# Two blocks of a language model in one kernel: the order of transposes and logits in both attention stages

## The reference, cut to what matters

```python
logits = einsum('bqhd,bqkhd->bhqk', qb, kg) * scale      # (+ bias or forget term in block 2)
logits = where(valid, logits, -inf)
p      = softmax(logits)                                   # kind c: one more term, the sink, in the sum
out    = einsum('bhqk,bqkhd->bqhd', p, vg)
```

## Time and profile before

| what | value |
|---|---|
| median of three runs | 981.58 us |
| the profiled execution | 983.36 us, of which the span (first to last instruction) is 981.6 us |
| mean granted TensorE clock | 0.952 of full |
| PE busy | 865.4 us, 88% |
| DVE busy | 503.7 us, 51% |
| ACT busy | 388.2 us, 40% |
| POOL busy | 81.4 us, 8% |
| attention rounds of stage 1 | about 158 to 231 us of the span |
| attention rounds of stage 2 | about 601 to 731 us of the span |

### The profile page before, as it was taken

The page is one execution under the profiler, slowest core; times in us unless marked ns, Lnnn a source line. Parts: engine busy times, 40 slices in busy tenths (PEclk is TensorE's granted clock), DMA queues, the critical chain, the costliest instruction groups (busy, mean ns, idle before and its releaser), DMA issues.

```text
span 981.6 us, 14775 instructions
## 1 busy us (share of the span) xinstructions
PE 865.4 (88%) x5993; PEld 716.8 (73%) x5993; DVE 503.7 (51%) x781; ACT 388.2 (40%) x523; POOL 81.4 (8%) x105
## 2 busy tenths in 40 slices
PE   4899998999996896668666699999989999999996
PEld 4899798999984441333312499988878799999995
DVE  5798667645655210111100644455557557666674
ACT  5333544464322111111111625545552356656462
POOL 1122001120000000000000000211115000000000
PEclk9999999899998898898888689999999999999998
DMA  6755463244569699999999736443352827564711
GB/s 205 258 184 196 147 233 112 87 172 172 172 252 424 279 423 422 422 422 422 422 421 353 135 122 161 162 140 118 118 141 86 288 81 254 170 214 139 242 47 43
DMA packets 93875, 217.50 MB, mean 222 GB/s; under 512 B 16455, under 2 KB 43973, under 8 KB 81537
## 3 DMA queue, kind: packets, MB, share of 16 engines
q1 hardware_dynamic: 93137, 215.32, 60.8%
q10 hardware_dynamic: 576, 1.18, 0.4%
q0 software_dynamic: 112, 0.30, 0.3%
HBM read 215.44 MB, written 1.34 MB: 221 GB/s over the span
## 4 chain that ended last, share of the span: by engine, by line
PE 63%; DMA 16%; DVE 10%; ACT 4%; issue 3%; SPq 3%; POOL 0%; DVEq 0%; ACTq 0%
PE ps L742 15%; PE ps L744 15%; PE ps L743 14%; DMA moe_ring<-in_w_expert_in 14%; PE ps L1045 6%; PE ps L979 5%; DVE w_lo L1408 3%; ACT w_hi L1130 1%; DMA stage<-in_w_in 1%; PE ps L904 1%; PE ps L958 1%; DMA stage_b<-in_w_up 1%; PE ps L889 1%; SPq L623 1%; PE ps L994 1%
## 5 line engine op out<-in xcount | busy, mean ns | idle before, releaser
L742 PE MATMUL ps<-x_hi,w_hi 128*128 128x256 f32 x1008 | 290.8, 288 | 6.3 <-DVE w_lo L1408 4.3
L743 PE MATMUL ps<-x_lo,w_hi 128*128 128x256 f32 x1008 | 287.8, 285 | 0.0
L744 PE MATMUL ps<-x_hi,w_lo 128*128 128x256 f32 x1008 | 287.7, 285 | 0.0
L742 PEld LDWEIGHTS ps<-x_hi,w_hi 128*128 128x128 f32 x1008 | 196.3, 195 | 9.2 <-DVE w_lo L1408 5.7
L743 PEld LDWEIGHTS ps<-x_lo,w_hi 128*128 128x128 f32 x1008 | 196.1, 195 | 0.3
L744 PEld LDWEIGHTS ps<-x_hi,w_lo 128*128 128x128 f32 x1008 | 195.9, 194 | 0.0
L1408 DVE TENSOR_TENSOR w_lo<-stage,w_hi 128x2048 fp32r<-128x2048 f32 (+2 forms) x72 | 162.1, 2291 | 56.1 <-ACT w_hi L1130 54.4
L1130 ACT ACTIVATE w_hi<-stage 128x2048 fp32r<-128x2048 f32 (+2 forms) x74 | 133.1, 1849 | 63.1 <-PE ps L744 55.8
L979 PE MATMUL ps<-moe_ring,qk 128*32 128x512 f32 x448 | 72.5, 739 | 41.4 <-DMA moe_ring<-in_w_expert_in 41.4
L979 PEld LDWEIGHTS ps<-moe_ring,qk 128*32 128x32 f32 x448 | 17.2, 131 | 82.5 <-DMA moe_ring<-in_w_expert_in 47.9
L742 PE MATMUL ps<-w_hi,x_hi 128*128 128x512 f32 (+2 forms) x176 | 66.5, 378 | 3.4 <-DVE x_lo L1415 1.8
(11 more groups left out here) (306 smaller groups left out, 1412.1 us busy)
## 6 DMA issues: line engine op xcount, KB each, us to landing
moe_ring<-in_w_expert_in SPq DMA_DIRECT2D x56, 1024.0 KB, 18.6
stage<-in_w_in SPq DMA_DIRECT2D x24, 2048.0 KB, 7.9
moe_ring<-in_w_expert_out SPq DMA_DIRECT2D x16, 1024.0 KB, 21.3
stage_b<-in_w_up SPq DMA_DIRECT2D x12, 1024.0 KB, 8.0
stage<-in_w_down SPq DMA_DIRECT2D x11, 1024.0 KB, 5.2
stage<-in_w_up SPq DMA_DIRECT2D x10, 1024.0 KB, 9.2
up_odd<-in_w_expert_in SPq DMA_DIRECT2D x8, 1024.0 KB, 26.9
down_odd_a<-in_w_expert_out SPq DMA_DIRECT2D x8, 1024.0 KB, 21.8
```

Of the source, the lines that this page charges most:

```text
L742: mm(out, still[0], moving[0], start=first, stop=False)
L743: mm(out, still[0], moving[1], start=False, stop=False)
L744: return mm(out, still[1], moving[0], start=False, stop=last)
```

## The change

In both loops of `schedule()` the step pt(h-1) now stands ahead of qk(h):

```diff
     for h in range(HEADS + 1):
+        if h >= 1:
+            at("pt", h - 1)
         if h < HEADS:
             at("qk", h)
-        if h >= 1:
-            at("pt", h - 1)
         if h == 1:
             at("mix", 2)
             at("mix", 3)
@@
     for h in range(heads + 1):
+        if h >= 1:
+            at("pt", HEADS + h - 1)
         if h < heads:
             at("qk", HEADS + h)
-        if h >= 1:
-            at("pt", HEADS + h - 1)
         if h < heads and gates:
             steps.append(gates.pop(0))
```

## The result

| | before | after |
|---|---|---|
| median of seven runs each | 982.79 us | 988.58 us |
| ratio, with 95% interval | | 1.0057 [1.0042, 1.0071] |
| profiled execution (span) | 983.36 us (981.6) | 987.48 us (985.8) |
| forecast | | 986.0 us, +0.45% (range 983.2 to 989.0) |

The ratio gives a loss of 5.6 us (4.1 to 7.0). The interval reaches to both sides of the 0.5% inside which I had put the larger chance; 0.40 stood for slower. The median lies 2.6 us over the forecast; 1.2 us of that is the median of the kernel before, which was 981.58 us in three runs and is 982.79 in seven. The two profiled executions differ by 4.1 us, nearly the 4.45 us of the sum.

A forecast was written before the change was run, and what follows sets the result against it. Both stages were taken as bound by PE with few gaps, a longer chain becoming stage 2's bound. 0.25 + 4.3, less 0.1, gave +4.45 us on the 981.58 us median: 986.0 us, range 983.2 to 989.0.

The forecast's parts named there:

- The closed loop: Stage 2, kind c: chain between odd heads' transposes becomes the bound, 17.14, 16.87, 16.88 and 17.27 us.
- The extra turn of the tile shape: Stage 2, PE: one more tile-shape turn a round, 0.17 to 0.18 us; 1.26 us over rounds 1 to 7.
- Stage 1: Round 4: PE's new wait for POOL, less the removed wait for the copy, nets +0.25 us without building up.
- the wait of 1.07 us: Stage 1, round 4: PE waits 1.07 us for POOL's normalized head 3 before its transposes.
- Stage 2: From the first logits to head 15's transposes: extra turns, then the longer chain, together +4.3 us.
- Carried to the end in full: After head 15's transposes, everything to the end shifts by the full loss; stage 1's 0.25 us likewise delays expert loads.
- The rival that the turn is free: Stage 2: the extra turn costs nothing, so +2.5 us in all, 984.1 us; chance 0.14.
- the rival of a gain: Both stages: copy waits of 1.2 us go and the new wait doesn't come, 980.4 us; chance 0.08.
- the four waits: Stage 2: PE waits for POOL before the transposes four times, 0.8 to 1.2 us each.
- the rival of the clock: Stage 2: new waits halve PE's clock, 994 us, or 988 with one spell; chance 0.14 with any other slow slip.

The follow-up runs named there:

- act_copy_last: Changed kernel, but ACT alone copies the transposes behind the next head's exponentials as before; ratio to the kernel before 1.0064 [1.0042, 1.0086].
- after_split_apart: Changed kernel with the two weight-split halves one before each gate fill in both stages; ratio to the kernel before 1.0013 [0.9997, 1.0028].
- ab_rounds_only: Kernel before with the new order in rounds 1 to 7 of stage 2 only; ratio to the kernel before 1.0023 [1.0008, 1.0038].
- best_candidate: Kernel before with ACT's copy first in both stages and split halves one before each gate fill in stage 2 only; 979.65 us against 983.10, 0.9965.
- after_split_stage2: Changed kernel with the split halves one before each gate fill in stage 2 only; ratio to the kernel before 1.0003 [0.9994, 1.0013].
- after_again: The changed kernel measured again, no edit; ratio to the kernel before 1.0059 [1.0039, 1.0079].
- stage2_only: Kernel before with the new order in stage 2 alone; ratio to the kernel before 1.0060 [1.0040, 1.0081].
- act_copy_first: Kernel before, but ACT alone copies the transposes ahead of the next head's exponentials; ratio to the kernel before 0.9991 [0.9977, 1.0005].
- split_apart_act_first: Kernel before with ACT's copy first and split halves one before each gate fill in both stages; ratio to the kernel before 0.9985 [0.9972, 0.9998].
- split_apart_stage2: Kernel before with only the split halves one before each gate fill in stage 2; ratio to the kernel before 1.0024 [1.0012, 1.0036].
- stage1_only: Kernel before with the new order in the first loop (stage 1) only; ratio to the kernel before 1.0007 [0.9994, 1.0020].

## Why the prediction was right, point by point

- **The closed loop** (POOL, transposes, logits, DVE's mask, split, next head) was forecast at 68.16 us over four turns and took 732.56 - 664.66 = 67.90. The last turn was 0.18 us shorter than I had it (17.09 for 17.27), of which I had taken off 0.1. The way from the first logits to the transposes of head 7 was 63.02 us, for 664.58 - 601.46 = 63.12. The chain as the bound is shown by act_copy_last (a longer link, a longer loop) and after_split_apart (a shorter link, no wait).
- **The extra turn of the tile shape**, the term with no row of its own, was taken at 0.18 us a round. It is 0.18 to 0.19 (rounds 2 to 7 of ab_rounds_only, and the 2.65 us between best_candidate and after_split_stage2). I counted one too many: of rounds 1 to 7 only six have it, which is why they cost 1.17 us and not 1.26. The Trainium skill, TensorEngine Tiling (Array Packing), Key Properties, says that changing the tiling mode drains TensorE. The trace agrees: a group of another shape starts 0.07 us before the end of the last one, one of the same shape 0.24 us.
- **Stage 1**: forecast +0.25, D1 shows +0.26 to +0.28. POOL's chain was right to 0.01 us; the wait of 1.07 us was not, since PE came up to 1.1 us later to that point than I had it. What PE lost ahead of the point it did not wait there, so the sum came out all the same.
- **Stage 2**: forecast +4.3, D2 shows +3.95 to +3.99.
- **Carried to the end in full**: in the profiled executions the rest from the transposes of head 15 took 253.19 us before and 253.24 us after. For the 0.25 us of stage 1 this isn't shown: from the transposes of head 7 to the first logits of stage 2 the 13 executions take 370.7 to 373.5 us (before 372.69, after 372.01), a spread ten times as large.
- **The rival that the turn is free** fell with ab_rounds_only, and the rival of a gain with the four waits. In the rival of the clock I judged the rounds right: from 675 to 730 us the granted clock is 1.00 in all four kernels with the loop (after, after_again, stage2_only, act_copy_last).
- **Where I misjudged**: that rows 11 show how much the clock stands at the end of stage 2. That was one execution. Of the 13 in the table it fell there in six: stage2_only, ab_rounds_only, act_copy_last, act_copy_first, split_apart_act_first and split_apart_stage2. In stage2_only (PE, PEld, DVE, ACT, POOL, granted clock):

```profile
732.00:734.00 2.00, 1.44 (x4) 0.69 (x4) 0.00 (x0) 0.31 (x1) 0.00 (x0) 0.66 0.18 64
734.00:736.00 2.00, 0.98 (x5) 1.00 (x5) 0.43 (x1) 1.93 (x2) 0.00 (x0) 0.50 0.00 0
736.00:738.00 2.00, 2.00 (x12) 2.00 (x11) 1.60 (x1) 2.00 (x2) 0.00 (x0) 0.50 0.00 0
738.00:740.00 2.00, 2.00 (x13) 2.00 (x13) 1.38 (x2) 0.16 (x1) 1.75 (x1) 0.64 0.00 0
```

and in the changed kernel at the same place:

```profile
732.00:734.00 2.00, 0.67 (x4) 0.49 (x5) 0.43 (x1) 0.54 (x2) 0.41 (x1) 1.00 0.77 290
734.00:736.00 2.00, 0.98 (x6) 0.61 (x6) 0.43 (x1) 1.25 (x2) 0.00 (x0) 1.00 0.00 0
736.00:738.00 2.00, 2.00 (x19) 2.00 (x18) 0.93 (x1) 2.00 (x2) 0.00 (x0) 1.00 0.00 0
```

Between 736 and 738 us the first does 12 matmuls, the second 19. The rest of the span is 253.0 to 253.5 us where the clock stands. Where it fell it is 254.8 to 255.8, and 257.5 in split_apart_stage2, whose last av waits 1.7 us longer. That is about 2 us, in kernels with the old and the new order alike.

**What stays open.** The stages account for 4.2 us, the timed runs show 5.6 (4.1 to 7.0), and the two repeats of the stage 2 order as much, so some 1.4 us may be real. The runs of one kernel spread over 2 to 6 us. The fall of the clock at the end of stage 2 is worth 2 of them, the stretch between the stages up to 2.8. The mean clock of the timed runs points to the clock for a part. A straight line through the 23 runs of the kernel before (0.946 to 0.955, 985.98 to 980.32 us) gives 0.48 us for 0.001 of mean clock. The 12 repeats lie 0.0017 lower, so an estimate from these numbers is 0.8 us. It doesn't settle the matter: within the seven first runs of the changed kernel a lower clock does not go with a longer time, and why the clock should fall more often in this kernel, no run shows.

## What to carry to other kernels

When a wait moves ahead of work that another engine needs, look for the closed chain it makes and add up its links over one turn. If the sum exceeds the turn of the bounding engine, the chain becomes the bound, and each link in it, even on an idle engine, is paid in full. Here one round earlier on the consumer's engine (ACT) was good and on the producer's (PE) bad: take such a change apart by engine before keeping or dropping it.

## What the runs showed of the hardware

- A change of tile shape between neighbouring groups on TensorE (128*64, 64*128, 128*128) cost 0.18 to 0.19 us, of it 0.17 in the overlap of the last matmul with the next (0.07 for 0.24 us). The order of such groups is not free.
- At the end of stage 2 PE has two or three waits of 0.8 to 1.0 us within 4 us (in split_apart_stage2 one of 2.5 among them). Behind them the granted clock fell to 0.50 in six of 13 executions and stood at 1.00 in seven, also between executions with the same three waits (before and stage1_only stood, act_copy_first and stage2_only fell). With one wait of 0.7 to 0.9 us every 17 us, in the loop of the four kernels above, it never fell.
